# A two-layer decoder trunk: the embedding gate's eight blocks as four pairs by seven products, two regular up-projection blocks ahead of them, and token sums taken from x without its bias

## The reference, cut to what matters

```python
def hybrid_layer(x, p_i, ...):                     # two layers, one after the other
    ...                                            # three mixers, gates, output projection
    x = layer_norm(ALPHA * x + merged @ w_out, ln1_g, ln1_b)
    f_gate, f_up = jnp.split(x @ w_ffn_in, 2, axis=-1)            # (512, 1024) @ (1024, 2 * 2816)
    ffn = (jax.nn.silu(f_gate) * f_up) @ w_ffn_out
    ple = jax.nn.sigmoid(x @ w_ple_gate) * (p_i @ w_ple_proj)     # (512, 1024) @ (1024, 1024)
    return layer_norm(ALPHA * x + ffn + ple, ln2_g, ln2_b)
```

## Time and profile before

| | |
|---|---|
| median of 3 runs | 1786.07 us (1785.73 to 1786.78) |
| the profiled execution, its own time | 1786.35 us |
| its span, first to last instruction | 1784.6 us |
| busy in the span: TensorE, VectorE, ScalarE, GpSimd | 1762.5, 1248.9, 944.4, 850.6 us |
| granted TensorE clock, mean | 0.998 of full speed |

### The profile page before, as it was taken

How to read it: one execution, slowest core, us unless ns; L and a number is a source line. 1 busy time by engine, 2 the same in 40 slices (tenths; PEclk the granted TensorE clock), 3 DMA queues, 4 the chain that set the end, 5 groups by cost and what they waited for, 6 DMA issues and landing times.

```text
span 1784.6 us, 28654 instructions
## 1 busy us (share of the span) xinstructions
PE 1762.5 (99%) x9966; PEld 1538.7 (86%) x9966; DVE 1248.9 (70%) x2413; ACT 944.4 (53%) x1841; POOL 850.6 (48%) x458
## 2 busy tenths in 40 slices
PE   9999999999999999999999999999999999999997
PEld 9888888878779999988898888888787799999886
DVE  6379988867778888513363899887778788884133
ACT  4544777844455555422244557787444565654222
POOL 5446943344443434354434578434443444444542
PEclk9999999999999999999999999999999999999999
DMA  5332211223333333233333321112232333332431
GB/s 192 99 94 92 60 60 60 63 73 102 95 118 95 110 105 103 88 118 107 95 99 102 98 83 60 60 60 64 80 105 94 107 107 97 117 96 83 130 98 68
DMA packets 47077, 166.62 MB, mean 93 GB/s; under 512 B 5472, under 2 KB 5728, under 8 KB 46944
## 3 DMA queue, kind: packets, MB, share of 16 engines
q1 hardware_dynamic: 46080, 163.60, 29.6%
q10 hardware_dynamic: 864, 1.28, 0.2%
HBM read 162.76 MB, written 2.10 MB: 92 GB/s over the span
## 4 chain that ended last, share of the span: by engine, by line
PE 78%; issue 9%; POOL 5%; DVE 5%; ACT 2%; DMA 0%; POOLq 0%; DVEq 0%; SPq 0%; ACTq 0%
PE banks L1133 20%; PE banks L1135 20%; PE banks L1134 20%; POOL sb_wl L604 5%; PE banks L1184 4%; PE banks L1185 4%; PE banks L1186 4%; PE banks L1240 2%; PE banks L1287 2%; DVE banks L1682 1%; PE banks L1271 1%; DVE sb_hconv L1977 1%; PE banks L1216 1%; PE banks L1270 0%; POOL sb_csq_sum L635 0%
## 5 line engine op out<-in xcount | busy, mean ns | idle before, releaser
L604 POOL TENSOR_TENSOR sb_wl<-sb_wraw,sb_wh 128x1024 fp32r<-128x1024 f32 x223 | 547.5, 2459 | 657.1 <-ACT sb_wh L732 637.4
L1133 PE MATMUL banks<-sb_xh,sb_wh 128*128 128x512 f32 (+1 forms) x1184 | 428.6, 362 | 3.9 <-POOL sb_wl L604 2.9
L1135 PE MATMUL banks<-sb_xh,sb_wl 128*128 128x512 f32 (+1 forms) x1184 | 411.9, 348 | 0.0
L1134 PE MATMUL banks<-sb_xl,sb_wh 128*128 128x512 f32 (+1 forms) x1184 | 411.2, 347 | 0.0
L732 ACT ACTIVATE sb_wh<-sb_wraw 128x1024 fp32r<-128x1024 f32 x215 | 227.1, 1057 | 300.4 <-PE banks L1135 184.1
L1133 PEld LDWEIGHTS banks<-sb_xh,sb_wh 128*128 128x128 f32 x1184 | 224.9, 190 | 30.8 <-issue 5.1
L1135 PEld LDWEIGHTS banks<-sb_xh,sb_wl 128*128 128x128 f32 x1184 | 224.3, 189 | 29.3
L1134 PEld LDWEIGHTS banks<-sb_xl,sb_wh 128*128 128x128 f32 x1184 | 225.2, 190 | 18.3
L1134 PE MATMUL banks<-sb_t_lo,sb_wh 128*128 128x256 f32 x640 | 181.1, 283 | 0.0
L1133 PE MATMUL banks<-sb_t_hi,sb_wh 128*128 128x256 f32 x640 | 181.1, 283 | 0.0
L1135 PE MATMUL banks<-sb_t_hi,sb_wl 128*128 128x256 f32 x640 | 181.1, 283 | 0.0
(11 more groups left out here) (345 smaller groups left out, 3952.2 us busy)
## 6 DMA issues: line engine op xcount, KB each, us to landing
...
```

The costliest lines, as they stand in the source:

```text
L604: nc.gpsimd.tensor_tensor(wl[:, slot(t), :], wraw[:, t % 2, :], wh[:, slot(t), :].bitcast(F32), ALU.subtract).then_inc(lo_ready, 1)
L1133: nc.tensor.matmul(out, wh_, xh_, start=start, stop=False, skip_group_check=onto)
L1134: nc.tensor.matmul(out, wh_, xl_, start=False, stop=False, skip_group_check=onto)
L1135: return nc.tensor.matmul(out, wl_, xh_, start=False, stop=stop, skip_group_check=onto)
```

## The change

The gate's blocks are taken in four pairs (`NG`) and made by seven products as well, as pairs 0 to 3 of now 24 pairs; the up-projection's pairs 2 to 21 follow as pairs 4 to 23. Pairs 0 and 1 of the up-projection are the regular blocks (`NR` = 2) and stand first, right after the norm; nothing regular stands at the end. The token sums are made from `u` before its bias is added: T2, T3 and T4 take the bias as a column in each of four instructions of 256 columns, and T1 needs none as its two operands share it. The bias is added to `u` by ScalarE later, between the units. For a gate pair one instruction over two blocks (512 columns) each does the tanh, the product with `pp` and the sum into `u`. Banks are numbered anew.

```diff
-T_PG = T_PP + 4
-T_FI = T_PG + DK
-T_FO = T_FI + 2 * FK
+T_R = T_PP + 4
+NR, NG = 2, DK // 2
+NS = NG + FK - NR
+T_S = T_R + 2 * NR
+T_FO = T_S + 2 * NS
...
-TAIL_BANKS = ((5, 6), (7, 4))
+R_BANKS = ((2, 3), (1, 4))
+T3, T2, T4, T1 = 1, 2, 3, 0
...
 def ffn_steps():
 
-    act, dve, pool = [], [(-6, ("sum3", 0)), (-4.6, ("sum1", 0))], []
+    act = [(-9, ("t high", T3)), (-8.9, ("gate", 0)), (-8.8, ("t high", T2)), (-4.4, ("gate", 1)), (-1.4, ("t high", T4)),
+           (1.2, ("t high", T1)), (10, ("hidden high", 0)), (17, ("hidden high", 1))]
+    act += [(1.6 + 0.6 * j, ("bias", j)) for j in range(DK)]
...
```

ScalarE, the regular blocks' and bias steps, and the gate pairs' tanh:

```diff
+                    elif what == "t high":
+                        act.wait_ge(t_made, layer * T_MADE[T1] + T_MADE[n])
+                        nc.scalar.activation(t_hi[:, n], t_raw[:, n], ACT.Copy,
+                                             scale=-1.0 if n in (T2, T4) else 1.0).then_inc(t_high, 1)
+                    elif what == "bias":
+                        act.wait_ge(x_ready, layer * 16 + (DK + n + 1))
+                        act.wait_ge(t_made, layer * T_MADE[T1] + T_MADE[T1])
+                        nc.scalar.activation(u[:, n], u[:, n], ACT.Identity, bias=column("l1b", n)).then_inc(x_raw, 1)
+                    elif what == "gate":
+                        gate(T_R + 2 * n, first, R_BANKS[n][0], th[:, n, :], 0.0, ffn_th)
...
+                    elif what == "th first" and n < NG:
+                        act.wait_ge(c11_ready, at + (n + 1))
+                        act.wait_ge(c21_ready, at + (n + 1))
+                        nc.scalar.activation(psum[:, G_BANK, :], psum[:, G_BANK, :], ACT.Tanh,
+                                             scale=0.5).then_inc(th_first, 1)
```

```diff
-                for k in range(0, DK, 2):
-                    if k == 2:
-                        pe.wait_ge(pp_out, layer * DK + DK)
-                    if k == 6:
-                        pe.wait_ge(h_done, layer * (DK + FK) + (2 + 2))
-                    side_by_side(T_PG + k, PG_BANK[k], xh, xl, x_block if k == 0 else lambda kk: None)
+                side_by_side(T_R, R_BANKS[0][0], xh, xl, x_block)
+                pe.wait_ge(pp_out, layer * DK + DK)
+                for c in range(2):
+                    project(T_R + 2 + c, first, xh, xl, DK, [R_BANKS[1][c]])
...
-                for q in range(NS, FK):
...
-                    project(T_FI + 2 * q, first, xh, xl, DK, [TAIL_BANKS[q - NS][0]])
-                    if q == NS:
-                        unit(NU - 1)
-                    project(T_FI + 2 * q + 1, first, xh, xl, DK, [TAIL_BANKS[q - NS][1]])
-
                 for j in range(DK):
                     pe.wait_ge(u_ready, layer * 16 + (DK + j + 1))
+                    if j < 2:
+                        pe.wait_ge((c21_ready, c11_ready)[j], layer * NS + NS)
                     for part in range(PARTS):
...
+                        if j == 0 and part == 0:
+                            unit(NU - 1)
```

```diff
+                    elif what == "t" and n == T3:
+                        for k in range(KH):
+                            v.scalar_tensor_tensor(t_raw[:, T3, k], u[:, KH + k, last_half], bias_step[:, k:k + 1],
+                                                   u[:, k, last_half], ALU.add, ALU.subtract).then_inc(t_made, 1)
...
+                    elif what in ("product first", "product second") and n < NG:
+                        c = int(what == "product second")
+                        g = psum[:, A_BANK[n % 2] if c else G_BANK, :].rearrange("p (b t) -> p b t", b=2)
+                        dve.wait_ge((th_first, th_second)[c], at + (n + 1))
+                        v.scalar_tensor_tensor(g, g, 1.0, pp[:, 2 * n:2 * n + 2, HALF * c:HALF * c + HALF], ALU.add,
+                                               ALU.mult).then_inc((product_first, product_second)[c], 1)
```

More of the change, by code:

```diff
@@ L251, in ffn_steps @@
         at = {kind: UNIT_AT[(kind, j)] for kind in PRODUCT}
+        late = 1 if j < NG else 0
         act += [(at["a11"] + 1, ("m1", j)), (at["s3"] + 1, ("m7", j)), (at["s2"] + 1, ("u2", j)),
-                (at["a12"] + 2, ("th first", j)), (at["a22"] + 3, ("high first", j)), (at["s4"] + 1, ("th second", j)),
-                (at["s4"] + 3, ("high second", j))]
+                (at["a12"] + 2 + late, ("th first", j)), (at["s4"] + 1, ("th second", j))]
+        if j >= NG:
+            act += [(at["a22"] + 3, ("high first", j)), (at["s4"] + 3, ("high second", j))]
         dve += [(at["a12"] + 1, ("c11", j)), (at["a22"] + 1, ("c21", j)), (at["s1"] + 1, ("c22", j)),
-                (at["a22"] + 2, ("product first", j)), (at["a22"] + 4, ("low first", j)),
+                (at["a22"] + 2 + late, ("product first", j)), (at["a22"] + 4, ("low first", j)),
                 (at["s4"] + 2, ("product second", j)), (at["s4"] + 4, ("low second", j)),
@@ L570, in _ @@
                 first = layer * TILES
-                with sp.Fori(first // 2 + (layer == 0), (first + T_FI) // 2 + 1) as m:
+                with sp.Fori(first // 2 + (layer == 0), (first + T_S) // 2 + 1) as m:
                     for t in range(2):
@@ L684, in _ @@
                                             ALU.subtract).then_inc(a11_low if kind == "a11" else lo_ready, 1)
-                for t in range(T_FI + 2 * NS, T_FO):
-                    low(t, first)
                 tiles(layer, T_FO, TILES)
@@ L1102, in _ @@
-                for k in range(PARTS * DK):
-                    if T_FO + k + LEAD < TILES or layer < L - 1:
+                    nc.scalar.activation(wh[:, t % WS, :], wraw[:, t % 2, :], ACT.Copy).then_inc(hi_ready, 1)
+                high(T_R + LEAD, first)
+                for _, (what, n) in FFN_ACT:
+                    ffn(what, n)
+                for k in range(PARTS * DK):
+                    if k == 0:
+                        ffn("tile", LEAD)
+                    elif T_FO + k + LEAD < TILES or layer < L - 1:
@@ L2150, in _ @@
+                for _, (what, n) in FFN_DVE:
+                    ffn(what, n)
+                steps.end("V_FI", V_FI)
                 steps.stage(layer * V_LAYER + VS_LN2)
@@ L2196, in weight_tiles @@
     tiles.append(padded(feature_tiles(w_ple_proj, 2 * P)))
-    tiles.append(feature_tiles(w_ple_gate, P))
-    fi = feature_tiles(w_ffn_in, P)
-    for j in range(NS):
-        (a11, a12), (a21, a22) = [np.split(fi[b:b + 1], 2, axis=2) for b in (j, FK + j)]
+    pg, fi = feature_tiles(w_ple_gate, P), feature_tiles(w_ffn_in, P)
+    for j in range(NR):
+        tiles += [fi[j:j + 1], fi[FK + j:FK + j + 1]]
+    pairs = [(pg[2 * j:2 * j + 1], pg[2 * j + 1:2 * j + 2]) for j in range(NG)]
+    pairs += [(fi[j:j + 1], fi[FK + j:FK + j + 1]) for j in range(NR, FK)]
+    for pair in pairs:
+        (a11, a12), (a21, a22) = [np.split(block, 2, axis=2) for block in pair]
         tiles += [np.concatenate([a21, a12], axis=2), np.concatenate([a11, a22], axis=2)]
-    for j in range(NS, FK):
-        tiles += [fi[j:j + 1], fi[FK + j:FK + j + 1]]
     down = w_ffn_out.reshape(FK, P, DK, P).transpose(2, 1, 0, 3)
```

272 lines of the change are left out of this document (135 added, 137 removed).

## The result

The changed kernel takes 1788.70 us, the kernel before in the same comparison 1786.14 (20 runs each); the ratio is 1.0014, 95% interval 1.0007 to 1.0020. It is slower by 2.6 us, within what I had called no change; the forecast was 1787.5 us, +1.4 to the kernel before. The profiled execution has a span of 1786.7 us, 2.1 more than before.

What follows compares the result with a forecast made beforehand. TensorE, busy for 1762.5 of 1784.6 us, was taken as the bound. Per layer 5.5 us of new waits against 4.8 saved, 2 x (5.5 - 4.8) = +1.4 us, gave about 1787.5 us; range 1780.5 to 1792.5.

Steps and rivals of the forecast that it cites:

- no change: Whole kernel: a time from 1782.5 to 1789.6 us, within about 0.2% or 3.6 us; chance 0.51.
- TensorE's saving, 4.8 us per layer: Gate stage: eight gate tiles become 28 units and start waits go; 268.99 becomes 264.2 us if no unit waits.
- The start: First unit at 516.3 instead of 539.7; new 256-column sums 0.40 us each; VectorE through T4's low part at 521.2.
- The waits: TensorE's new waits around the first gate pairs, together 5.5 us per layer; rival at 1787.5 us, chance 0.50.
- a22, on GpSimd: Pair 0: its low part waits for VectorE's low T1 and sum3 of pair 1, until 524.1; 1.4 us.
- a11 of pair 2: Needs the bank of pair 0's last step, which ends at 540.1 where a11 should start at 538.9; 1.5 us.
- the walk: Each engine's order set beside measured durations, with 0.1 to 0.2 us per semaphore; it gave 5.5 us lost per layer.
- The rule: SBUF port: GpSimd enters at VectorE's next change only if it asked under 0.25 us before, else at its next pause.
- VectorE is behind its units by 2.5 us ... After it the slack returns: Pairs 2 and 3: a11 waits 1.5 and 0.3 us, restarts 0.2; then 0.76 us of tanh waiting per pair covers.
- fourth rival: VectorE bounds all four gate pairs; 0.5 us more lost in each of pairs 2 and 3, 1789.5 us; chance 0.08.
- The second: Rival: the port costs little, units nearly run through; 1.0 us lost per layer, 1778.5 us; chance 0.22.
- The third: Rival: GpSimd gets in after each VectorE instruction; 7.3 us lost per layer, 1791.2 us; chance 0.20.

Runs made afterwards that it cites:

- run 12: The eleventh's order, with GpSimd making the low parts of a11, a12 and a22 of the four gate pairs on 16 of 512 columns only: 1777.64 us.
- runs 8 to 11: VectorE's order moved: eighth; changed kernel with pair 0's last step earlier and hidden low parts later; eighth plus these moves; eleventh. 1783.17, 1788.81, 1782.92, 1782.66 us.
- run 7: Changed kernel with GpSimd making the low parts of a12 and a22 of pair 0 on 16 of 512 columns only: 1784.83 us.
- fourth: Changed kernel with VectorE's T4, T1 and sum 3 of pair 2 earlier and T1's low part behind hidden block 1; nothing left out: 1782.67 us.
- eighth: The fourth's order, with VectorE's corners c11, c21 and c22 of pair 0 moved earlier: 1783.17 us.
- eleventh: The eighth with pair 0's last step earlier, hidden blocks' low parts later, and T1's low part ahead of hidden block 1: 1782.66 us.
- 1: Changed kernel with VectorE making token sums T4 and T1 and their low parts on 32 of 256 columns only: 1783.64 us.
- 4 to 6: On the changed kernel: the fourth's whole reorder, only its move of sum 3 of pair 2, only its token-sum moves: 1782.67, 1786.22, 1785.62 us.
- 2: Changed kernel with ScalarE adding the bias to 8 of 512 columns in each of its eight steps: 1788.36 us.

## Why the prediction was right, and where it was not

**TensorE's saving, 4.8 us per layer: right.** With the waits gone the stage is 264.7 us (run 12), 4.3 less than before with 0.5 of waits left. It also bears out the durations on which it rests, 0.227 and 0.120 us a matmul as in the rows. By the isolated gap in "TensorE: Matmul & The Clock Gate" (the Trainium skill, on the back-to-back issue gap) the exchange would have been worth some 3 us more over the two layers, an estimate; run 12 does not show them, and the trace disagrees with it.

**The start: right.** First unit at 516.03 (forecast 516.3, and the whole layer lies 0.30 earlier), four 256-column sums in 1.67 us, so 0.40 each as estimated, VectorE through the low part of T4 at 520.9 (521.2).

**The waits: the sum nearly right, its terms less so.** 6.0 us per layer against 5.5:

| | forecast | measured |
|---|---|---|
| s2, on copy m1 | 0.7 | 0.6 |
| a12, on GpSimd | 1.4 | 1.2 |
| a22, on GpSimd | 1.4 | 0.8 |
| s1, on copy u2 | none | 0.8 |
| s3 of pair 1, on c21 | none | 0.65 |
| a11 of pair 2 | 1.5 | 1.6 |
| a11 of pair 3 and restarts | 0.5 | 0.35 |

Two waits were missing, 1.45 us, and one was 0.6 too large; with the small differences 1.55 were too little and 1.05 too much. That the sum came within 0.5 is in part luck. The remaining 0.5 us per layer are most of the 1.2 us between +1.4 and +2.6.

**The step that failed in the walk: when GpSimd gets the port.** The rule was that GpSimd is let in at VectorE's next change of instruction only if it asked less than 0.25 us before, else at VectorE's next pause. It held at 518.80: GpSimd was passed over between T1 and the low part of T4. It failed next. a22's low part could be asked for from 522.2 on, when a12's was done, some 0.8 us before VectorE's next change; sum 3 of pair 1 followed without a pause, and GpSimd was let in ahead of it, near 523.0 instead of 524.1. So a22 waited 0.8 instead of 1.4, and sum 3, which the walk let run undisturbed, took 1.1 us longer. ScalarE waits for that sum, the copy u2 stands behind ScalarE's high part, and so s1 waits 0.8 where the walk had nothing.

**The step that had the right waits for a wrong reason: "VectorE is behind its units by 2.5 us ... After it the slack returns".** Its waits, 1.5 at a11 of pair 2 and 0.5 behind it, were measured as 1.6 and 0.35. But for the slack I had VectorE's own steps, 8.2 us in a gate pair, and 0.76 us of waiting for tanh in the later pairs as cover. VectorE is in fact busy through all of gate pairs 2 and 3. From one corner c21 to the next (starts of L2120: 540.15, 550.58, 560.38) it takes 10.43 and 9.80 us, where TensorE's pair takes 10.08: 8.2 of its own, 1.5 of port, and in the first of the two a hidden block's low part. So its arrears hardly shrink before the up-projection's pairs come, and a reordering that removes one wait in this stretch can get another (runs 8 to 11). This is near the fourth rival, to which I gave 0.08: over the gate pairs VectorE has no time to spare, and the port is why. Its price of 0.5 us in each of pairs 2 and 3 did not come in the changed kernel; a wait in pair 4 came only in the reordered ones.

**The rivals.** The second (the port costs little, 1778.5) is refuted by the rows: GpSimd's 5.47 us, and the waits of a12 and a22 on it. Run 12, with the port nearly free but another order, took 1777.6; in the change's order only the low parts of a12 and a22 were freed (run 7), and 3.9 us per layer were still lost, not 1.0. The third (the port changes hands at every instruction, s1 2.7 us late) came true in two of its three places: the low part of T1 and sum 3 of pair 1 each waited 1.0 to 1.1 us for a low part, the low part of T4 did not. s1 waited 0.8 and not the 2 us that I had named as its sign. In the fourth, eighth and eleventh runs GpSimd was let in at the first change each time, where my rule would have kept it out longer.

**What is settled and what not.** Shown: the gain (12), that VectorE's steps at the start make three of the waits (1), what its order is worth (4 to 6), what GpSimd's low parts and the port cost together (7, 12), and that ScalarE only hands waits on (2). Not settled: when VectorE gives up the port. "SBUF — State Buffer" (the Trainium skill, on the two separate sides) has it as a lock held for the whole instruction. The rows agree with that much; the change's row at 518.80 shows besides that the lock can pass from one VectorE instruction to the next over a waiting GpSimd. I have no run that says when.
